# Experts' gate and up weights as f16 halves, split one expert ahead, in a hybrid decoder layer

## The reference

```
eid_s = eid[order]; counts = jnp.bincount(eid, length=N_EXPERTS)      # 32 experts
padded = (counts + MOE_BLK - 1) // MOE_BLK * MOE_BLK                  # blocks of 128 rows
def expert_block(args):
    xb, e = args
    return (jax.nn.silu(xb @ w_g[e]) * (xb @ w_u[e])) @ w_d[e]
y = ybuf.reshape(...)[dest] * gate_s[:, None]
return jax.ops.segment_sum(y, tok_s, num_segments=n_tok)
```

## Time and profile before

| | us |
|---|---|
| median of three runs | 2752.8 (2750.51 to 2752.84) |
| the profiled execution, its own time | 2750.93 |
| its span, from first to last instruction | 2749.3 |
| experts' stage, from its first gate matmul to the end | about 1,420 |
| one block of the experts' stage on TensorE | 17.71 |

### The profile page before, as it was taken

One profiled execution on the slowest core, in us unless ns is written; L12 is line 12 of the kernel. 1 busy time (PEld: TensorE's weight loads), 2 busy tenths in 40 slices (PEclk: granted clock), 3 DMA queues, 4 the chain that ended last, 5 costly groups with the idle time before them and its releaser, 6 DMA issues.

```text
span 2749.3 us, 49924 instructions
## 1 busy us (share of the span) xinstructions
PE 2643.6 (96%) x14252; PEld 1820.9 (66%) x14253; DVE 1716.2 (62%) x3920; ACT 1391.3 (51%) x3046; POOL 798.8 (29%) x825
## 2 busy tenths in 40 slices
PE   4999999999999999996699999999999999999997
PEld 2455555555555555553588888888888888888886
DVE  5677777777777777776454455545655444546633
ACT  7666555565555566553344445445545333435533
POOL 1122323232322222331232333323223323333232
PEclk9999999999999999998799999999999999999999
DMA  8376555556655555656556677667767665667763
GB/s 315 82 166 166 156 160 158 152 157 165 163 152 160 154 156 164 166 138 167 187 169 189 186 236 244 200 196 224 235 186 232 205 183 153 194 180 237 235 181 54
DMA packets 546395, 495.22 MB, mean 180 GB/s; under 512 B 411787, under 2 KB 411948, under 8 KB 545340
## 3 DMA queue, kind: packets, MB, share of 16 engines
q1 hardware_dynamic: 517516, 406.08, 49.2%
q0 software_dynamic: 28848, 88.77, 13.8%
HBM read 309.74 MB, written 87.88 MB: 145 GB/s over the span
## 4 chain that ended last, share of the span: by engine, by line
PE 89%; DVE 3%; DMA 3%; ACT 2%; issue 1%; SPq 1%; POOL 1%; POOLq 0%; DVEq 0%; ACTq 0%
PE psB L1676 15%; PE psA L1676 15%; PE psG L574 11%; PE psF L1676 7%; PE psG L1676 7%; PE psE L574 6%; PE psF L574 6%; PE psD L574 6%; PE psC L574 6%; PE psH L574 3%; PE psC L1684 1%; PE psD L1684 1%; PE psE L1691 1%; DMA xg<-hn_rows,slots 1%; DMA slots<-slot_table 1%
## 5 line engine op out<-in xcount | busy, mean ns | idle before, releaser
L574 PE MATMUL psG<-wi_all,both_xT 128*128 128x512 f16 x1536 | 345.2, 382 | 10.9 <-DMA both_xT<-x 10.9
L574 PEld LDWEIGHTS psG<-wi_all,both_xT 128*128 128x128 f16 x1536 | 148.7, 98 | 188.2 <-DMA both_xT<-x 11.1
L1600 POOL DMA_INDIRECT xg<-hn_rows,slots x80 | 99.2, 1240 | 544.0 <-DMA slots<-slot_table 389.4
L1676 PE MATMUL psB<-up_hi,gT_hi 128*128 128x512 f32 x632 | 254.4, 402 | 0.0
L1676 PE MATMUL psA<-gate_hi,gT_hi 128*128 128x512 f32 x632 | 247.3, 391 | 3.1 <-ACT gT_hi L1796 1.7
L1812 DVE TENSOR_TENSOR down_lo<-wi_all,down_hi 128x512 fp32r<-128x512 f32 x256 | 157.0, 686 | 147.1 <-ACT down_hi L1770 147.1
L1676 PE MATMUL psB<-up_hi,gT_lo 128*128 128x512 f32 x632 | 247.6, 392 | 0.0
L1676 PE MATMUL psA<-gate_hi,gT_lo 128*128 128x512 f32 x632 | 247.3, 391 | 0.0
L1676 PE MATMUL psA<-gate_lo,gT_hi 128*128 128x512 f32 x632 | 247.0, 391 | 0.0
L1676 PE MATMUL psB<-up_lo,gT_hi 128*128 128x512 f32 x632 | 246.4, 390 | 0.0
L1796 ACT ACTIVATE gT_hi<-psC 128x512 fp32r<-128x512 f32 x80 | 47.8, 597 | 384.8 <-PE psC L1684 384.8
(11 more groups left out here) (320 smaller groups left out, 5777.2 us busy)
## 6 DMA issues: line engine op xcount, KB each, us to landing
wi_all<-in_w_gate SPq DMA_DIRECT2D x32, 2048.0 KB, 9.5
wi_all<-in_w_up SPq DMA_DIRECT2D x32, 2048.0 KB, 12.9
wi_all<-in_w_down SPq DMA_DIRECT2D x32, 2048.0 KB, 11.7
xt<-in_x SPq DMA_DIRECT2D x32, 512.0 KB, 3.7
um<-u_rows SPq DMA_DIRECT2D x64, 256.0 KB, 2.7
out_rows<-h SPq DMA_DIRECT2D x32, 512.0 KB, 3.0
xres<-in_x SPq DMA_DIRECT2D x31, 512.0 KB, 4.1
hn_rows<-xres SPq DMA_DIRECT2D x31, 512.0 KB, 2.9
```

What stands on the lines that cost most here:

```text
L574: m = nc.tensor.matmul(ps, left[:, l, k, :], weights.half(r, k, n, width), start=(k == opens and j == 0), stop=(k == closes and j == 2))
L1600: pool.indirect_dma_start(xg[:], None, hn_dram, bass.IndirectOffsetOnAxis(ap=slots[:, 0, 0:1], axis=0), bounds_check=SEQ + P - 1).then_inc ...
L1676: m = nc.tensor.matmul(ps[:, :], l[:, k, :], r[:, r_k[n], :], start=(n == 0 and j == 0), stop=(n == len(l_k) - 1 and j == 2))
```

## The change

Gate and up weights and the gathered rows become f16 halves, as in the mixer. Since f16 has a small range, each expert's gate and up weights are multiplied by a power of two. It is taken from a bound on the sum of their absolute values: ScalarE sums up each partition (`sum_up`, one Abs activation over 128x4096 with an accumulated output), GpSimd takes the largest over the partitions (`bound_of`, an all-reduce), VectorE makes the power and its inverse in five small steps (`scales`). The inverse goes into SiLU's scale and into the product. Down stays in fp32r.

The split of expert e+1's gate and up is done during expert e's second block, into a second set of halves; the sums during its first block, behind SiLU. The split of down stays in its own expert's first block. Weights are cut in two chunks of 128x2048 in place of eight of 128x512. Raw gate and up have two places each and are loaded two experts ahead. Every expert is given at least two blocks (with these inputs each has them already). The walk takes two experts in each turn of its loop, so that the parity of the places is fixed in the code.

The core of the diff:

```
-        raw = {n: wi_flat[...] for j, n in enumerate(("gate", "up", "down"))}
+        place = [wi_flat[:, j * 4096:(j + 1) * 4096]... for j in range(5)]
+        raw = {"gate": (place[0], place[3]), "up": (place[1], place[4]), "down": (place[2], place[2])}
...
-        step(v.tensor_scalar(blocks_of[:, counts], blocks_of[:, E:], 1, None, ALU.max))
-        step(v.tensor_scalar(blocks_of[:, 0:1], blocks_of[:, 0:1], 2, None, ALU.max))
+        step(v.tensor_scalar(blocks_of[:, counts], blocks_of[:, E:], 2, None, ALU.max))
...
-    hi = {n: sb(f"{n}_hi", [P, 8, 512], F32R) for n in raw}
+    hi = {n: [sb(f"{n}_hi_{p}", [P, 8, 512], F16) for p in range(2)] for n in SCALED}
-    gT_hi, gT_lo = sb("gT_hi", [P, KD, P], F32R), sb("gT_lo", [P, KD, P], F32R)
+    gT_hi, gT_lo = sb("gT_hi", [P, KD, P], F16), sb("gT_lo", [P, KD, P], F16)
...
     def sync(sp):
+        def next_loads(e, p, down=True):
+            for n in SCALED:
+                split_up(n, e)                  # waits until hi and lo of gate/up e are made
+                load_expert(sp, n, e + 2, p)
+            if down:
+                split_up("down", e)
+                load_expert(sp, "down", e + 1, p)
+        sp.wait_ge(summed, 2)
+        for n in SCALED:
+            load_expert(sp, n, 1, 1)
         mixed(sp)
-        with sp.Fori(1, E) as e:
-            for n in raw:
-                sp.wait_ge(hi_s[n], 8 * e)
-                sp.wait_ge(lo_s[n], 8 * e)
-                load_expert(sp, n, e)
+        with sp.Fori(0, (E - 2) // 2) as pair:
+            next_loads(pair * 2, 0)
+            next_loads(pair * 2 + 1, 1)
...
     def gpsimd(pool):
+        def bound_of(e, p):
+            pool.wait_ge(summed, 2 * (e + 1))
+            hold(pool, held)
+            pool.partition_all_reduce(most(p), sums(p), P, RMAX).then_inc(most_s, 1)
...                                             # at the end of an expert's second block:
+            if isinstance(i, int) and i == 1 and not last:
+                bound_of(e + 1, 1 - p)
...
     def tensor(pe):
-                if fresh:
-                    pe.wait_ge(hi_s[name], e * 8 + r_k[n] + 1)
-                    pe.wait_ge(lo_s[name], e * 8 + r_k[n] + 1)
+            if first:
+                weights("gate", e)              # one wait for hi and lo of the whole matrix
...
     def scalar(act):
+        def block_(e, i, b, p, r, last):
+            if not (known and b < 2):
+                copy_y(b)
+            if not (known and b == 0):
+                turn(b)
+            silu(b, p)
+            if first and not last:
+                sum_next("gate", p, r, b)
+            if second and not last:
+                split("gate", e + 1, 1 - p)
+            turn_x(b + 1)
+            if first and not last:
+                sum_next("up", p, r, b)
+            if first:
+                split_down(e, b)
+            if second and not last:
+                split("up", e + 1, 1 - p)
```

More of the change, by code:

```diff
@@ L177, in build @@
         rows_of_y = ksb("rows_of_y", [P, 1], I32)
+        rt_stat = ksb("rt_stat", [P, 9], F32)
+        own = ksb("own", [P, 2, 12], F32)
         with ExitStack() as ctx:
@@ L1637, in block_ @@
             gather()
-            if known:
+            if known and b < 2:
                 pool.wait_ge(cleared, 3)
@@ L1700, in down, with weights, block_ @@
             for half, ps in enumerate((psF, psG)):
-                split_mm(ps, range(KE), (aT_hi, aT_lo), (hi["down"], lo["down"]), [2 * k + half for k in range(KE)],
-                         False).then_inc(y_ps, 1)
-        def block_(e, i, b, first):
+                split_mm(ps, range(KE), (aT_hi, aT_lo), (hi["down"][0], lo["down"][0]),
+                         [2 * k + half for k in range(KE)]).then_inc(y_ps, 1)
+        def weights(n, e):
+            pe.wait_ge(hi_s[n], CHUNKS * (e + 1))
+            pe.wait_ge(lo_s[n], CHUNKS * (e + 1))
+        def block_(e, i, b, p, r, last):
             static0 = isinstance(b, int) and b == 0
+            first, second = isinstance(i, int) and i == 0, isinstance(i, int) and i == 1
             pe.wait_ge(xgT_hi, 2 * (b + 1))
@@ L1765, in scalar, with sum_up, sum_next, split @@
         s = nc.scalar
-        def split(n, e):
-            act.wait_ge(raw_in[n], 16 * (e + 1))
-            for k in range(8):
-                s.activation(hi[n][:, k, :], raw[n][:, k, :], ACT.Copy).then_inc(hi_s[n], 1)
+        def sum_up(n, p, r, junk):
+            act.wait_ge(raw_in[n][p], 16 * (r + 1))
+            s.activation(junk, raw[n][p].rearrange("p k n -> p (k n)"), ACT.Abs, accum_out=sums(p, n)).then_inc(summed, 1)
+        def sum_next(n, p, r, b):
+            if not (isinstance(b, int) and b == 0):
+                act.wait_ge({"gate": gate_ps, "up": up_ps}[n], b)
+            sum_up(n, 1 - p, r + p, hi[n][1 - p][:].rearrange("p k n -> p (k n)").bitcast(BF16))
+        def split(n, e, p):
+            act.wait_ge(step_s, SCALE_STEPS * (e + 1))
+            for c in range(CHUNKS):
+                s.activation(chunk(hi[n][p], c), chunk(raw[n][p], c), ACT.Copy, scale=power(p, n)).then_inc(hi_s[n], 1)
+        def split_down(e, b):
+            act.wait_ge(raw_in["down"][0], 16 * (e + 1))
+            if not (isinstance(b, int) and b == 0):
+                act.wait_ge(y_ps, 2 * b + 4)
+            for c in range(CHUNKS):
+                s.activation(chunk(hi["down"][0], c), chunk(raw["down"][0], c), ACT.Copy).then_inc(hi_s["down"], 1)
         def copy_y(b):
@@ L1782, in silu @@
                 act.wait_ge(act_s, b)
-            s.activation(gated[:], psA[:, :], ACT.Silu).then_inc(silu_s, 1)
+            s.activation(gated[:], psA[:, :], ACT.Silu, scale=inverse(p, "gate")).then_inc(silu_s, 1)
         def turn(b):
@@ L1835, in turn_x, with block_ @@
                 dve.wait_ge(xgT_hi, 2 * b + h + 1)
-                v.tensor_tensor(gT_lo[:, 4 * h:4 * h + 4, :].rearrange("p k c -> p (k c)"), ps[:, :],
-                                gT_hi[:, 4 * h:4 * h + 4, :].rearrange("p k c -> p (k c)").bitcast(F32),
-                                ALU.subtract).then_inc(xgT_lo, 1)
+                hold(dve, held)
+                v.scalar_tensor_tensor(gT_lo[:, 4 * h:4 * h + 4, :].rearrange("p k c -> p (k c)"), ps[:, :], hn_scale,
+                                       gT_hi[:, 4 * h:4 * h + 4, :].rearrange("p k c -> p (k c)"),
+                                       ALU.mult, ALU.subtract).then_inc(xgT_lo, 1)
+        def block_(e, i, b, p, r, last):
+            known = isinstance(b, int)
+            first, second = isinstance(i, int) and i == 0, isinstance(i, int) and i == 1
+            if not (known and b < 2):
+                copy_y(b)
+            if second and not last:
+                scales(e + 1, 1 - p)
+            if not (known and b == 0):
+                turn(b)
+            if second and not last:
+                split("gate", e + 1, 1 - p)
+            product(b, p)
+            turn_x(b + 1)
+            if first:
+                split_down(e)
+            if second and not last:
+                split("up", e + 1, 1 - p)
         v.memset(slots[:], 0).then_inc(cleared, 1)
@@ L1845, in vector @@
         dve.sem_inc(y_dve, 3)
-        halves(dve, split, copy_y, product, turn, turn_x)
+        split("gate", 0, 0)
+        turn_x(0)
+        split("up", 0, 0)
+        total = walk(dve, block_)
+        copy_y(total)
+        turn(total)
+        copy_y(total + 1)
     return dict(sync=sync, tensor=tensor, scalar=scalar, gpsimd=gpsimd, vector=vector)
```

185 lines of the change are left out of this document (104 added, 81 removed).

## The result

The changed kernel takes 2878.8 us (median of 4 runs, 2877.9 to 2879.6), the kernel before 2752.8 beside it: a ratio of 1.0459, 95% interval 1.0441 to 1.0478. The forecast was 2732 us and the range ended at 2790. The change makes the kernel slower by 126 us.

A forecast was written before the change was run, and what follows sets the result against it. TensorE was taken to bound the kernel, busy 1402.7 of 1415.0 us in the experts' stage. From 2750.9: minus 41.7, plus 6 (VectorE's chain), 9 (gathers) and 8 (start) gave 2732 us; range 2704 to 2790.

The forecast's parts named there:

- TensorE's gain, -41.7: Experts' stage: f16 gate and up matmuls make each block 0.53 us shorter, 41.7 us over 79 blocks.
- VectorE's chain, 6 us: Expert's second block: TensorE waits for `gT_lo`, 0 to 0.4 us, taken as 0.2 in each of 31 experts.
- The second block's gather: Gather behind the all-reduce: issued from 22.4 on the block count, landed 4.5 us later at 26.9, 1.1 us early.
- The rival of 0.08: All-reduce delays the second block's gather 6.5 us in 16 two-block experts: 104 us, 2821 in all; chance 0.08.
- The rival's second half: By the skill's rule, the gather's issue at 22.4 would wait for `down_lo` until 23.8: 1.4 us against 1.1 slack.
- The gather behind `gate_lo`, 9 us: Gather for an expert's next block, after a table read behind `gate_lo`: 0 to 2.3 us late, taken as 0.3, 31 times.
- The start, 8 us: Start of the experts' stage: expert 1's loads delay first table read and gather by 6 us, second block's gather by 2.

The follow-up runs named there:

- e1_sums: The changed kernel with ScalarE summing up right behind gate, ahead of the next rows' `gT_hi`: 2767.2 us, ratio 1.0049.
- e6_uneven: The changed kernel with up summed ahead of `gT_hi` and all three matrices' halves made in pieces of 1024, 1024 and 2048: 2755.0 us, ratio 1.0004.
- e2_called: The changed kernel with down's load waiting until GpSimd's queue has gone past the gather of that expert's first rows: 2832.0 us, ratio 1.0273.
- e5_arrived: The changed kernel with down's load waiting until the expert's first rows have arrived: 2774.3 us, ratio 1.0079.
- e4_start: The changed kernel with the two loads for the second expert waiting for expert 0's all-reduce: 2879.2 us, ratio 1.0460.
- e7_start: The changed kernel with an unneeded all-reduce ahead of the first one and the second expert's loads waiting for the first rows: 2866.7 us, ratio 1.0419.
- e3_eight: The changed kernel with down's halves made in eight instructions of 512 on both engines again: 2909.2 us, ratio 1.0554.

## Why the prediction was wrong

**TensorE's gain, -41.7: right.** Gate takes 5.19 us and a clean block 17.16 against 17.18 forecast; 78 periods gave 42.2.

**VectorE's chain, 6 us: right in place, in size by luck.** I took 0.2 us in each of 31 experts. Three-block experts' second blocks took 0.42 more, 5.8 us; in two-block ones it was covered by the stall. e1_sums brings it out there (0.62): uncovered, the term is 16 us and not 6. e6_uneven removes it. The steps came 0.32 apart, not 0.19.

**The second block's gather, the step that failed.** The prediction's chain for it was exact up to the gather's start: 22.4 on its count is 5.2 into the second block, and the gather starts at 5.2 to 5.7. It failed in the next sentence, "landed 4.5 us later": in the two-block experts the rows land 8.6 to 10.1 us behind the gather's start. The sum had nothing for this wait; the runs show 6.8 us in each of 16 experts, 109 us in all. The rival of 0.08 had the root, the all-reduce, and the place, 16 experts. Its route was another: the copies of the shift were to wait until 23.8, and they got through at 18.4 (0.19 us each). That its 104 us lie so near the 109 measured is luck. The rival's second half, that `down_lo` holds the gather's issue, was the right one. What turned me away from it was one row: gathers of 1097 ns at the median beside splits of 4.9 us. The rule that I set that row against (the Trainium skill, page "SBUF — State Buffer", section "SBUF: two separate sides", the box on VectorE blocking DMA) gave the right time: the issue was held until `down_lo` ended, at 6.6. The median had hidden the lock in the trace of the kernel before. Taken one by one, 42 of its 78 gathers start inside a run of such splits, and these take up to 2152 ns, while the 36 others take 1057 to 1074; their ends stand at steps of 0.60 us, the length of a piece, 0.95 behind a piece's end. Even the encounter with a load is there: nine gathers are held to the last piece of `gate_lo`, whose end also releases the load of gate, and their rows land 11.1 to 11.6 us into the block, where the 33 others land by 8.4. A group's median is no evidence on a case that the group mixes with others.

And I had priced the rule at 1.4 us late against 1.1 of slack, as if lateness cost its own length. The end of `down_lo` also releases down's load, so a held gather comes out behind it, and the 0.3 us became 4.4. TensorE's clock then made it 6.9 (below).

**The gather behind `gate_lo`, 9 us: wrong place, too small.** No first block lost any. The loss stands in the third blocks, 32.8 us, from a table read that lands with down's load (e2_called, e5_arrived) and a gather that then comes out behind the load of up. My chain, with two blocks in an expert, didn't contain it.

**The start, 8 us: 13 measured, for another reason.** Of the 13, 3.1 lie in the mixer: its last table scatter starts at 1312.4 in the kernel before and at 1315.5 in the changed one. It moves from one execution to the next, 1313.3 to 1318.9 in the runs here, so little can be read from it. I had the first all-reduce hidden ahead of the mixer's last DMAs. It ran 10.5 us behind its configuration. e4_start, e7_start: some 5.5 of these without any load, 5 more beside 4 MB of loads. A further 9 us went inside expert 0, where I had 2; e1_sums leaves 2.2 of them, so they were the second block's stall again.

A slip that changes nothing: the sum of 2732 is 2734 against the median of the runs, not 2733.

**What isn't settled.** Which boundaries between pieces let a gather through: one between two of 2048 does, those of eight of 512 did up to 3.5 us into a run in the kernel before, and from 3.2 us on not in e3_eight. And what makes the first all-reduce late: it comes 5.5 to 6.9 us behind its configuration in the five runs without the two loads in flight, 8.3 to 10.9 in the seven with them, and no row shows what GpSimd does in that time.

## What to carry to other kernels

Where a transfer and a load are both released by the same event, ask which of them is issued first, and by how much: here a load of 2 MB issued 0.7 us ahead made the rows 4.4 us later. Let the load wait for the arrival of the small transfer on the critical path; a wait on the instruction that issued it isn't enough, since the queue runs on. Before a row is set against a rule, look at its instances beside the thing that the rule speaks of.

## What the runs showed of the hardware

**A stall costs more than its length.** After the 4.4 us idle in the two-block expert above, the granted clock stayed at the lower level (0.50, 1.2 GHz) for some 5 us of full work, in the changed kernel by stretch:

```profile
1846.50:1857.30 10.80, 10.80 (x53) 5.09 (x52) 6.91 (x9) 7.24 (x6) 4.75 (x6) 1.00 0.27 84
1857.30:1861.80 4.50, 0.21 (x1) 0.00 (x0) 4.12 (x2) 2.13 (x2) 0.00 (x0) 0.79 1.01 342
1861.80:1863.20 1.40, 1.29 (x6) 1.29 (x7) 1.15 (x2) 0.14 (x1) 0.49 (x2) 0.50 1.05 272
1863.20:1866.00 2.80, 2.80 (x10) 2.32 (x9) 1.50 (x2) 2.64 (x3) 0.60 (x1) 0.50 1.03 309
1866.00:1870.60 4.60, 4.60 (x21) 3.52 (x19) 3.96 (x2) 2.97 (x3) 0.58 (x1) 0.92 0.91 337
```

The matmuls of down start 0.43 us apart until 1866.7 and 0.23 after it. Eight of them lose 1.6 us and the transposes 0.7: with the idle 4.4, 6.7 of the block's extra 6.9. Stalls of 0.4 us (second blocks of three-block experts) cost 0.4.

**An issue from GpSimd is not over when its queue has passed it**: e2_called's load went 1.5 us into the gather's issue of 2.38.

**The lock.** Gathers outside VectorE's splits are issued in 1.06 to 1.10 us; those held inside end 0.93 to 0.99 us behind the end of a piece or of the run, in each of the kernels here. Table reads (`slots<-slot_table`) that start inside such runs are not held: 30 of them in the changed kernel are issued in 0.58 to 0.62 us, as outside. The box of the Trainium skill named above speaks of VectorE's copies in a two-port mode, and these are none; the rule of the same section that the prediction names first, two SBUF inputs against a GpSimd instruction that reads SBUF, fits them, since the gather takes its row numbers from `slots` in SBUF and the table read takes none. The trace agrees with that rule in kind; that eight instructions back to back can hold a gather like one is beyond what the section says.
